# Moving GpSimd's Newton steps, weight splits and gate split within the steps of an attention loop

## The chip, the cores and the metric

The kernel runs on one core of a Trainium2 chip. The metric is the device time of one execution in microseconds (us), the median of the runs shown; lower is better.

## What is computed

One layer of a decoder trunk, batch 1, 512 tokens, width 1024, all in float32. Cut to what matters here:

```python
h = rms_norm(x, attn_norm)
(mq, mk, mv, nsq, kc, vc, ksl, vsl, kwn, vwn, ngate, mgate) = split(h @ w_in)
q_a = rms_norm(to_heads(mq, 8), moba_q_gain)      # each head of 64 is normalised by itself
k_a = rms_norm(to_heads(mk, 8), moba_k_gain)
y_a = moba_attention(q_a, k_a, to_heads(mv, 8))    # 8 heads, all causal blocks at this length
q_b = rms_norm(nsq in 8 heads, nsa_q_gain)
y_b = nsa_attention(q_b, ...)                      # 8 heads: compressed, selected and window branch
g_a, g_b = split(sigmoid(mgate))
x = x + (g_a * (y_a @ w_br_moba) + g_b * (y_b @ w_br_nsa)) @ w_o
x = x + (gelu(conv(rms_norm(x) @ w_up)) * lin) @ w_down
x = x + sigmoid(x @ w_ple_gate) * (p @ w_ple)
```

## The kernel before

Each engine (TensorE, VectorE, ScalarE, GpSimd, and SyncE for the DMA queue) has its own instruction stream, in an order written out by hand; semaphores join them. Every float32 matmul is done as three matmuls of a high and a low part (lines 1511 to 1513, in the helper `three`), so each weight has to be split: ScalarE copies a rounded high part, and VectorE or GpSimd subtracts it from the raw weight to get the low part.

The attention half is a loop over 100 steps t. A step is one block of 128 queries of one head and branch. Steps come in pairs of heads: pairs 0 to 3 have 8 steps each (t = 0, 8, 16, 24 are their first), pairs 4 to 7 have 17 each (first steps 32, 49, 66, 83). In step t TensorE computes `scores(t)`, transposes the probabilities of step t-3 (`turn_probs`, line 1660), and between them does a few matmul rows of other work:

- `project`: the projection h @ w_in of a *weight unit* w, four token tiles of 128 rows, 8 rows of k each. Unit w=3 is projected in steps 4 to 9, unit 4 in steps 12 to 17, unit 5 in 20 to 25, unit 6 in 28 to 35 and unit 7 in 43 to 58. Each unit gives the queries, keys and values of a later pair.
- `gate`: one of 16 column blocks of the merge gates.
- `turn_tile` (line 1571): the transposes of a normalised tile of queries and keys, in step TURN.

The other engines' part of a step:

- VectorE: `bias(t)` (line 1295, adds the bias strip and takes the minimum), `invert(t-1)` (line 1312), `sums` of squares (line 1229), `pt_low` (line 1330), `tile_low` (line 1281, low parts of the tile turned a step before), `w_low` (line 1171, even rows of the unit's weights), `normalise` (line 1262, of one tile), `guess` (lines 1146 to 1148, three small instructions that make a first guess of the inverse square roots of two tiles), `gate_low` (line 1187, the first half of a gate's low part), and every so often a copy of a finished output (line 1402).
- ScalarE: takes projected tiles from PSUM (line 830), `pt_high` (line 919), `tile_high` (line 883), `exp(t)` (line 894), a gate's tanh (line 926) and high part (line 1000), and the high parts of two rows of weights (line 835).
- GpSimd: `scale(t-1)` (lines 706 and 709, multiplies the probabilities by 1/sum), `split_gate` (line 674, the second half of a gate's low part), `split_unit` (line 670, the odd rows of the unit's weights), `v_low` (lines 683 and 688, the low part of the values), and `root` (lines 719 to 725): three Newton rounds of four instructions on 8 columns, which turn the guess into the inverse roots that `normalise` needs.

Planning dictionaries say in which step each thing falls. Before the change GUESS and ROOT are one: VectorE's `guess` and GpSimd's `root` stand in the same step. The roots of a unit are done in two halves of two token tiles. The step of ROOT is 0 and 2 for unit 2; 7 and 10, 15 and 18, 23 and 26 for units 3, 4, 5; 32 and 36 for unit 6; 51 and 59 for unit 7. `split_gate` stands in steps 4, 12, 20, 28, 40, 48, 57 and later. SPLIT has the rows 0-1, 2-3, 4-5, 6-7 of unit 3 in steps 1 to 4, of unit 4 in steps 9 to 12, of unit 5 in steps 17 to 20, of unit 6 in steps 25 to 28, of unit 7 in steps 41 to 44.

TensorE asks for row 7 of the weights (the last one that GpSimd splits) in the second step of a unit's projection, and before `turn_tile` it waits for `norm_done`. A projected tile is taken from PSUM only when the same tile of the unit before is normalised. SyncE's queue waits, in the step of `split_gate`, for both halves of that split before it loads the weights of the gate after.

Of the kernel before, what the change touches and what calls it, by code (L numbers as in the profile page):

```python
# [35 lines left out]
NGATE = 2 * D // P  # L36
# [36 lines left out]
def layer(nc, A, out):  # L73
# [20 lines left out]
    GATE, j = {}, 2  # L94
# [14 lines left out]
                j += 1  # L109
    gate_end = {j: t for t, (j, kts) in GATE.items() if kts[-1] == KT - 1}  # L110

    PROJ, SPLIT, VALUES, ROOT, TILE, TURN = {}, {}, {}, {}, {}, {}
    ROWS = NT * KT
    for w in range(2, W_UNITS):
        b0 = first_t[w - 2]
        if w == 2:
            start, counts, row = b0, (4, 4), ROWS - KT
        elif w < 6:
            start, counts, row = b0 - 4, (5, 6, 5, 5, 6, 5), 0
        elif w == 6:  # L120
            start, counts, row = b0 - 4, (4,) * 8, 0
        else:
            start, counts, row = b0 - 6, (2,) * 16, 0
        for a, count in enumerate(counts):
            PROJ[start + a] = (w, row, row + count)
            row += count
        split0 = b0 - 8 if w == 7 else b0 - 7
        for a in range(KT // 2):
            SPLIT[split0 + a] = (w, range(2 * a, 2 * a + 2))
        VALUES[start + len(counts)] = w  # L130
        ends = [t for t in sorted(PROJ) if PROJ[t][0] == w for r in range(*PROJ[t][1:]) if r % KT == KT - 1]
        for half in range(2):
            t = ends[2 * half + 1] + 1 if w > 2 else b0 + 2 * half
            ROOT[t] = (w, half)
            for a in range(2):
                TILE[t + 1 + half + 2 * a], TURN[t + 2 + half + 2 * a] = (w, 2 * half + a), (w, 2 * half + a)

    def segments(t):

# [58 lines left out]
    with ExitStack() as ctx:  # L198
# [453 lines left out]
        def _(pool):  # L652
# [19 lines left out]
            def split_gate(j):  # L672
                pool.wait_ge(g_hi, j + 1)
                pool.tensor_tensor(Gl[:, 4:8, :], graw[:, 4:8, :], Gh[:, 4:8, :].bitcast(F32), ALU.subtract).then_inc(g_lo[1], 1)  # L674
# [17 lines left out]
            def split_chunk(c):  # L692
                pool.wait_ge(w2_hi, c + 1)
                pool.tensor_tensor(W2l[:, c % RING, :], raw2[:, c % RING, :], W2h[:, c % RING, :].bitcast(F32),  # L694
                                   ALU.subtract).then_inc(w2_lo, 1)
# [12 lines left out]
                    h = cat(s["br"]) * HN + 2 * (s["n"] - 4) + s["e"]  # L708
                    pool.tensor_scalar(p_, p_, r, gsig[:, s["i"], h:h + 1], ALU.mult, ALU.mult).then_inc(scaled, 1)  # L709

            def root(w, half):

                number = 2 * (w - 2) + half
                c = slice(8 * half, 8 * half + 8)
                y, v, a = rq[:, c], st[:, 40:56][:, c], st[:, 60:76][:, c]
                pool.wait_ge(guess_done, number + 1)
                for i in range(3):
                    done = 12 * number + 4 * i
                    pool.tensor_tensor(a, y, y, ALU.mult).then_inc(root_done, 1)
                    pool.wait_ge(root_done, done + 1)  # L720
                    pool.tensor_tensor(a, a, v, ALU.mult).then_inc(root_done, 1)
                    pool.wait_ge(root_done, done + 2)
                    pool.tensor_scalar(a, a, -0.5, 1.5, ALU.mult, ALU.add).then_inc(root_done, 1)
                    pool.wait_ge(root_done, done + 3)
                    pool.tensor_tensor(y, y, a, ALU.mult).then_inc(root_done, 1)
                    if i < 2:
                        pool.wait_ge(root_done, done + 4)
# [36 lines left out]
            for t in range(T + 1):  # L764
                if t >= 1:
                    scale(t - 1)
                if t == T:
                    break
                for j, end in gate_end.items():
                    if t == end + 1 and j + 1 < NGATE:  # L770
                        split_gate(j + 1)
                if t in SPLIT:
                    split_unit(*SPLIT[t])
                if t in VALUES and VALUES[t] != 6:
                    v_low(VALUES[t])
                if t in ROOT:
                    root(*ROOT[t])
                if t in EARLY:
                    split_chunk(EARLY[t])

# [348 lines left out]
        def _(dve):  # L1129
# [116 lines left out]
            def guess(w, half):  # L1246

                c = slice(8 * half, 8 * half + 8)
                dve.wait_ge(ss_done, NT * (w - 2) + 2 * half + 2)
                if w > 2:  # L1250
                    dve.wait_ge(norm_done, norm_number(w - 1, 2 * half + 1))
                first_guess(rq[:, c], st[:, 40:56][:, c], st[:, 60:76][:, c], ss[:, c], 1.0 / DH, guess_done)
# [118 lines left out]
            for t in range(T + LAG):  # L1371
                n, k, w = (STEPS[t]["n"], STEPS[t]["k"], STEPS[t]["n"] + 2) if t < T else (NPAIR, 0, 0)
# [11 lines left out]
                    w_low(*SPLIT[t])  # L1384
                if t in TILE:
                    normalise(*TILE[t])
                if t in ROOT:
                    guess(*ROOT[t])
                for j, end in gate_end.items():
                    if t == end + 1 and j + 1 < NGATE:  # L1390
                        gate_low(j + 1)
# [15 lines left out]
            for mg in range(2):  # L1407
# [5 lines left out]
                for m in range(4):  # L1413
                    i = 4 * mg + m
# [7 lines left out]
                for m in range(4):  # L1422
                    i = 4 * mg + m
# [8 lines left out]
            for mg in range(2):  # L1432
                for m in range(4):
                    i = 4 * mg + m
# [48 lines left out]
            for mg in range(2):  # L1483
                for m in range(4):
                    i = 4 * mg + m
# [449 lines left out]
```

## Time and profile before

| | before |
|---|---|
| median of 3 runs | 942.68 us (942.12 to 945.08) |
| the profiled execution | 943.29 us |
| its span, first to last instruction | 941.3 us |
| TensorE busy | 894.5 us, 95% of the span |
| VectorE, ScalarE, GpSimd busy | 438.2, 410.6, 434.4 us |
| mean granted clock of TensorE | 0.985 |

The profiled execution is one run; its time is 2 us more than its span. Times inside the trace are from the span's start. An engine's idle time before an instruction is shown with what ended it, in square brackets.

### The profile page before, as it was taken

The numbers are of one execution on the slowest core, as the hardware profiler recorded it, in microseconds if no ns is written. First come the engines' busy times: TensorE is split into PE (matmuls) and PEld (weight loads), VectorE is DVE, ScalarE is ACT, GpSimd is POOL, SyncE is SP. The second block draws the span as 40 slices with busy tenths as digits, with TensorE's granted clock in tenths as the row PEclk, the third lists the DMA queues.
The fourth block names the chain that finished last, engine by engine and source line by source line (L and its number), as shares of the span: only waits on it lengthen the run. The fifth ranks groups of instructions, "written<-read, shape, count | busy, mean of one in ns | idle before, by whom it ended". The sixth has DMA issues, their size and how long they took to land.

```text
span 941.3 us, 13367 instructions
## 1 busy us (share of the span) xinstructions
PE 894.5 (95%) x4585; PEld 769.2 (82%) x4585; DVE 438.2 (47%) x965; ACT 410.6 (44%) x889; POOL 434.4 (46%) x557
## 2 busy tenths in 40 slices
PE   6898989998999799999999999999999999999998
PEld 6897888987889688878778788888888888888886
DVE  5718558658666464563431743333344441021134
ACT  4221546546565455572343474444444443232231
POOL 4633445535443433475446164444444445444450
PEclk7998999999999999999999999999999999999999
DMA  5744324224112122616653163333333233332213
GB/s 168 164 132 118 82 84 94 71 85 105 42 34 68 34 81 65 213 46 235 201 190 101 51 197 101 104 104 94 101 96 95 90 101 101 101 100 89 91 57 134
DMA packets 101365, 99.33 MB, mean 106 GB/s; under 512 B 15956, under 2 KB 76084, under 8 KB 101300
## 3 DMA queue, kind: packets, MB, share of 16 engines
q1 hardware_dynamic: 101247, 98.48, 35.7%
q8 instruction: 38, 0.62, 0.3%
q14 instruction: 27, 0.22, 0.1%
q10 hardware_dynamic: 53, 0.01, 0.0%
HBM read 87.58 MB, written 10.88 MB: 105 GB/s over the span
## 4 chain that ended last, share of the span: by engine, by line
PE 79%; DVE 9%; POOL 3%; issue 3%; ACT 3%; DMA 2%; SPq 1%; DVEq 0%; ACTq 0%; POOLq 0%
PE banks L1511 24%; PE banks L1512 23%; PE banks L1513 23%; PE banks L1660 2%; PE banks L1640 1%; PE banks L1639 1%; DVE plain_arena L1262 1%; PE banks L1571 1%; DVE split_arena L1281 1%; DMA plain_arena<-in_x_dram 1%; PE banks L1597 1%; DMA plain_arena<-in_w_in_dram 1%; POOL split_arena L670 1%; ACT split_arena L1000 1%; DVE split_arena L1187 1%
## 5 line engine op out<-in xcount | busy, mean ns | idle before, releaser
L1511 PE MATMUL banks<-split_arena 128*128 128x512 f32 (+4 forms) x1228 | 466.2, 380 | 17.1 <-POOL split_arena L670 7.2
L1513 PE MATMUL banks<-split_arena 128*128 128x512 f32 (+4 forms) x1228 | 455.4, 371 | 0.0
L1512 PE MATMUL banks<-split_arena 128*128 128x512 f32 (+4 forms) x1228 | 455.2, 371 | 0.0
L694 POOL TENSOR_TENSOR split_arena<-plain_arena,split_arena 128x512 fp32r<-128x512 f32 x184 | 241.2, 1323 | 254.4 <-ACT split_arena L935 235.1
L1511 PEld LDWEIGHTS banks<-split_arena 128*128 128x128 f32 x1228 | 232.3, 189 | 58.5 <-POOL split_arena L670 9.3
L1513 PEld LDWEIGHTS banks<-split_arena 128*128 128x128 f32 x1228 | 232.3, 189 | 35.5
L1512 PEld LDWEIGHTS banks<-split_arena 128*128 128x128 f32 x1228 | 232.7, 190 | 32.0
L935 ACT ACTIVATE split_arena<-plain_arena 128x512 fp32r<-128x512 f32 x184 | 113.0, 627 | 192.7 <-PE banks L1513 177.3
L1469 DVE SCALAR_TENSOR_TENSOR plain_arena<-banks,plain_arena 128x511 f32<-128x511 f32 x44 | 32.7, 743 | 133.2 <-ACT plain_arena L1040 133.2
L894 ACT ACTIVATE plain_arena<-plain_arena 128x128 f32<-128x128 f32 (+1 forms) x96 | 53.9, 562 | 65.0 <-DVE plain_arena L1295 64.5
L709 POOL TENSOR_SCALAR plain_arena<-plain_arena 128x128 f32<-128x128 f32 (+1 forms) x64 | 40.7, 636 | 72.7 <-DVE plain_arena L1312 72.5
L1295 DVE CUSTOM_DVE_ANT_0 plain_arena<-banks,plain_arena 128x128 f32<-128x128 f32 (+1 forms) x96 | 46.7, 487 | 51.0 <-PE banks L1640 50.2
L919 ACT ACTIVATE split_arena<-banks 128x128 fp32r<-128x128 f32 (+1 forms) x96 | 41.4, 431 | 64.1 <-PE banks L1660 55.4
L1330 DVE TENSOR_TENSOR split_arena<-banks,split_arena 128x128 fp32r<-128x128 f32 (+1 forms) x96 | 46.3, 482 | 16.4 <-ACT split_arena L919 14.9
L1660 PE MATMUL banks<-plain_arena 128*128 128x128 f32 x240 | 43.2, 278 | 6.9 <-POOL plain_arena L709 4.7
L1487 DVE TENSOR_TENSOR plain_arena<-banks,plain_arena 128x512 f32<-128x512 f32 x8 | 5.0, 684 | 86.5 <-PE banks L1513 86.5
L670 POOL TENSOR_TENSOR split_arena<-plain_arena,split_arena 128x384 fp32r<-128x384 f32 (+1 forms) x28 | 31.9, 1141 | 26.9 <-DVE split_arena L1164 14.6
L1040 ACT ACTIVATE plain_arena<-banks,plain_arena 128x512 f32<-128x512 f32 x44 | 30.7, 778 | 22.3 <-PE banks L1513 22.3
L674 POOL TENSOR_TENSOR split_arena<-plain_arena,split_arena 128x512 fp32r<-128x512 f32 x16 | 27.7, 1734 | 26.4 <-DVE split_arena L1182 14.4
L706 POOL TENSOR_SCALAR plain_arena<-plain_arena 128x128 f32<-128x128 f32 (+3 forms) x32 | 17.7, 553 | 46.5 <-DVE plain_arena L1312 46.4
L1660 PEld LDWEIGHTS banks<-plain_arena 128*128 128x128 f32 x240 | 28.6, 142 | 9.9 <-POOL plain_arena L709 6.9
L1471 DVE SCALAR_TENSOR_TENSOR plain_arena<-banks,plain_arena 128x510 f32<-128x510 f32 x44 | 33.0, 749 | 1.5
(170 smaller groups left out, 835.5 us busy)
## 6 DMA issues: line engine op xcount, KB each, us to landing
plain_arena<-in_w_up_dram SPq DMA_DIRECT2D x88, 256.0 KB, 3.1
plain_arena<-in_w_down_dram SPq DMA_DIRECT2D x44, 256.0 KB, 2.6
plain_arena<-in_w_in_dram SPq DMA_DIRECT2D x18, 512.0 KB, 4.5
plain_arena<-in_w_in_dram SPq DMA_DIRECT2D x32, 192.0 KB, 3.5
plain_arena<-in_x_dram SPq DMA_DIRECT2D x8, 512.0 KB, 5.2
gates<-plain_arena SPq DMA_DIRECT2D x16, 256.0 KB, 2.0
plain_arena<-skew SPq DMA_DIRECT2D x16, 256.0 KB, 4.0
plain_arena<-gates SPq DMA_DIRECT2D x16, 256.0 KB, 3.7
```

Source lines behind the costliest of these rows:

```text
L670: pool.tensor_tensor(Wl[:, kt, 0:c], raw[:, kt, 0:c], Wh[:, kt, 0:c].bitcast(F32), ALU.subtract).then_inc(w_lo[1], 1)
L694: pool.tensor_tensor(W2l[:, c % RING, :], raw2[:, c % RING, :], W2h[:, c % RING, :].bitcast(F32), ALU.subtract).then_inc(w2_lo, 1)
L709: pool.tensor_scalar(p_, p_, r, gsig[:, s["i"], h:h + 1], ALU.mult, ALU.mult).then_inc(scaled, 1)
L894: nc.scalar.activation(prob[:, t % 4, 0:nk], prob[:, t % 4, 0:nk], ACT.Exp, bias=mneg[:, t % 4:t % 4 + 1], scale=-1.0, accum_out=rsum[:, t ...
L919: nc.scalar.activation(PTh[:, s["u"] % 2, 0:i + 1, P * i:P * (i + 1)], PS[:, 4 + t % 2, 0:P * (i + 1)].rearrange("p (j q) -> p j q", j=i + ...
L935: nc.scalar.activation(W2h[:, c % RING, :], raw2[:, c % RING, :], ACT.Copy).then_inc(w2_hi, 1)
L1295: nc.vector.tensor_tensor_reduce(out=prob[:, t % 4, 0:nk], in0=PS[:, 2 + t % 2, 0:nk], in1=strip[:, n % 2, e, S - nk:S], scale=1.0, scalar ...
L1330: nc.vector.tensor_tensor(PTl[:, s["u"] % 2, 0:i + 1, P * i:P * (i + 1)], PS[:, 4 + t % 2, 0:P * (i + 1)].rearrange("p (j q) -> p j q", j= ...
L1511: nc.tensor.matmul(o, ah, bh, start=first, stop=False)
L1512: nc.tensor.matmul(o, ah, bl, start=False, stop=False)
L1513: return nc.tensor.matmul(o, al, bh, start=False, stop=last)
L1660: ins = nc.tensor.transpose(PS[:, 4 + t % 2, P * j:P * (j + 1)], prob[:, t % 4, P * j:P * (j + 1)], ident)
```

## The change

`root` gets a step of its own, one after `guess`. For the second half of units 2 to 5 it is cut in two: round 0 in the step after the guess, rounds 1 and 2 in the one after that (`late`). The steps of `normalise` (TILE) and `turn_tile` (TURN) follow:

| unit, half | guess | root, before and after | TILE before | TILE after |
|---|---|---|---|---|
| 2, first | 0 | 0, 1 | 1, 3 | 2, 4 |
| 2, second | 2 | 2, 3 and 4 | 4, 6 | 5, 7 |
| 3, first (4 and 5: 8 and 16 more) | 7 | 7, 8 | 8, 10 | 9, 11 |
| 3, second (4 and 5: 8 and 16 more) | 10 | 10, 11 and 12 | 12, 14 | 13, 15 |
| 6, first | 32 | 32, 33 | 33, 35 | 34, 36 |
| 6, second | 36 | 36, 37 | 38, 40 | 38, 40 |
| 7, first | 51 | 51, 52 | 52, 54 | 53, 55 |
| 7, second | 59 | 59, 60 | 61, 63 | 61, 63 |

TURN is one step after TILE, as before. Within a step GpSimd's order becomes scale, weights, values, root, gate's half, early chunk; before it was scale, gate's half, weights, values, root, early chunk. No instruction is added or removed.

```diff
@@ planning
         for half in range(2):
             t = ends[2 * half + 1] + 1 if w > 2 else b0 + 2 * half
-            ROOT[t] = (w, half)
+            GUESS[t] = (w, half)
+            late = 1 if half and w < 6 else 0
+            if late:
+                ROOT[t + 1], ROOT[t + 2] = (w, half, range(1)), (w, half, range(1, 3))
+            else:
+                ROOT[t + 1] = (w, half, range(3))
             for a in range(2):
-                TILE[t + 1 + half + 2 * a], TURN[t + 2 + half + 2 * a] = (w, 2 * half + a), (w, 2 * half + a)
+                TILE[t + 2 + late + 2 * a], TURN[t + 3 + late + 2 * a] = (w, 2 * half + a), (w, 2 * half + a)
@@ GpSimd
-            def root(w, half):
+            def root(w, half, rounds):
...
-                for i in range(3):
+                for i in rounds:
@@ GpSimd's loop over the steps
-                for j, end in gate_end.items():
-                    if t == end + 1 and j + 1 < NGATE:
-                        split_gate(j + 1)
                 if t in SPLIT:
                     split_unit(*SPLIT[t])
                 if t in VALUES and VALUES[t] != 6:
                     v_low(VALUES[t])
                 if t in ROOT:
                     root(*ROOT[t])
+                for j, end in gate_end.items():
+                    if t == end + 1 and j + 1 < NGATE:
+                        split_gate(j + 1)
@@ VectorE's loop over the steps
-                if t in ROOT:
-                    guess(*ROOT[t])
+                if t in GUESS:
+                    guess(*GUESS[t])
```

## Rows read from the trace of the kernel before

**Rows 1.** The page's first part: busy us (share of the span) xinstructions.
```profile
PE 894.5 (95%) x4585; PEld 769.2 (82%) x4585; DVE 438.2 (47%) x965; ACT 410.6 (44%) x889; POOL 434.4 (46%) x557
```

**Rows 2.** Waits of PE, 100 to 400 us: us in total, times, longest.
```profile
PE banks L1511 <- POOL split_arena L670: 7.2, 5, 1.7
```

**Rows 3.** Timeline of PE, 103 to 266 us: start, us, instruction, idle before.
```profile
120.01 0.44 PE L1511 MATMUL banks<-split_arena 128*128 128x384 f32 x1 [0.29 <-DVE split_arena L1171]
122.55 0.45 PE L1511 MATMUL banks<-split_arena 128*128 128x384 f32 x1 [1.75 <-POOL split_arena L670]
...
157.81 0.44 PE L1511 MATMUL banks<-split_arena 128*128 128x384 f32 x1 [1.67 <-POOL split_arena L670]
...
227.41 0.39 PE L1511 MATMUL banks<-split_arena 128*128 128x256 f32 x1 [1.65 <-POOL split_arena L670]
229.80 0.38 PE L1511 MATMUL banks<-split_arena 128*128 128x256 f32 x1 [0.55 <-ACT plain_arena L830]
241.87 0.38 PE L1511 MATMUL banks<-split_arena 128*128 128x256 f32 x1 [0.50 <-ACT plain_arena L830]
244.81 0.63 PE L1571 MATMUL banks<-plain_arena 128*128 128x128 f32 x4 [0.55 <-DVE plain_arena L1262]
...
256.37 0.63 PE L1571 MATMUL banks<-plain_arena 128*128 128x128 f32 x4
```

**Rows 4.** Timeline of POOL, steps 10 to 12, ahead of the wait at 157.81.
```profile
148.94 0.20 POOL L719 TENSOR_TENSOR plain_arena<-plain_arena 128x8 f32<-128x8 f32 x1 [0.31 <-DVE plain_arena L1148]
...
152.36 0.20 POOL L725 TENSOR_TENSOR plain_arena<-plain_arena 128x8 f32<-128x8 f32 x1
...
153.10 1.02 POOL L670 TENSOR_TENSOR split_arena<-plain_arena,split_arena 128x384 fp32r<-128x384 f32 x1
...
154.76 1.60 POOL L674 TENSOR_TENSOR split_arena<-plain_arena,split_arena 128x512 fp32r<-128x512 f32 x1
156.31 1.44 POOL L670 TENSOR_TENSOR split_arena<-plain_arena,split_arena 128x384 fp32r<-128x384 f32 x1
```

**Rows 5.** Timeline of ACT: high parts of rows 6 and 7, units 3 and 4.
```profile
118.49 0.92 ACT L835 ACTIVATE split_arena<-plain_arena 128x384 fp32r<-128x384 f32 x2
...
153.89 0.94 ACT L835 ACTIVATE split_arena<-plain_arena 128x384 fp32r<-128x384 f32 x2
```

**Rows 6.** Timeline of DVE: a guess, three normalises, and an invert (L1312).
```profile
147.45 1.21 DVE L1147 TENSOR_SCALAR plain_arena<-plain_arena 128x8 int32<-128x8 int32 x1
...
225.01 1.76 DVE L1262 TENSOR_TENSOR plain_arena<-plain_arena 128x512 f32<-128x512 f32 x1
...
243.98 0.69 DVE L1262 TENSOR_TENSOR plain_arena<-plain_arena 128x512 f32<-128x512 f32 x1 [2.54 <-POOL plain_arena L725]
...
252.22 0.16 DVE L1312 RECIPROCAL plain_arena<-plain_arena 128x1 f32<-128x1 f32 x1
...
321.49 0.69 DVE L1262 TENSOR_TENSOR plain_arena<-plain_arena 128x512 f32<-128x512 f32 x1 [4.61 <-POOL plain_arena L725]
```

**Rows 7.** Timeline of POOL, steps 59 to 62.
```profile
315.35 2.82 POOL L688 TENSOR_TENSOR split_arena<-plain_arena,split_arena 128x256 fp32r<-128x256 f32 x4 [1.64 <-ACT split_arena L866]
318.13 0.20 POOL L719 TENSOR_TENSOR plain_arena<-plain_arena 128x8 f32<-128x8 f32 x1
...
321.45 2.38 POOL L709 TENSOR_SCALAR plain_arena<-plain_arena 128x384 f32<-128x384 f32 x3
```

**Rows 8.** Timeline of PE: step 62, and a long wait near the start.
```profile
45.55 1.73 PE L1563 MATMUL banks<-plain_arena 128*128 128x128 f32 x8 [3.05 <-DVE plain_arena L1222]
...
322.69 0.90 PE L1660 MATMUL banks<-plain_arena 128*128 128x128 f32 x3 [4.66 <-POOL plain_arena L709]
...
324.67 1.05 PE L1571 MATMUL banks<-plain_arena 128*128 128x128 f32 x4
```

**Rows 9.** Windows: us, busy of PE, PEld, DVE, ACT, POOL, clock, DMA, GB/s.
```profile
322.30:325.70 3.40, 3.01 (x11) 2.62 (x12) 0.86 (x4) 0.98 (x3) 1.52 (x3) 0.50 0.00 0
...
332.50:336.00 3.50, 3.50 (x15) 3.21 (x15) 2.95 (x9) 3.00 (x7) 1.06 (x2) 0.51 0.13 50
```

More of the change, by code:

```diff
@@ L110, in layer @@
     gate_end = {j: t for t, (j, kts) in GATE.items() if kts[-1] == KT - 1}
-    PROJ, SPLIT, VALUES, ROOT, TILE, TURN = {}, {}, {}, {}, {}, {}
+    PROJ, SPLIT, VALUES, GUESS, ROOT, TILE, TURN = {}, {}, {}, {}, {}, {}, {}
     ROWS = NT * KT
```

## The prediction

> **What bounds the kernel now.** I read the busy times first, then TensorE's waits between 100 and 400 us (steps 0 to 64, the only part that the change touches), then for each wait that involves GpSimd the timelines of the four engines around it. TensorE is busy for 894.5 of 941.3 us [rows 1], so an edit on another engine is worth what it takes from TensorE's idle time, and no more. In the part touched, the largest kind of wait is the matmul's for a weight row that GpSimd splits: five times, 7.2 us together [rows 2]. Four of them are of one pattern, 1.65 to 1.75 us each, in the second step of the projection of units 3, 4, 5 and 6; three of the four stand in [rows 3], unit 5's is as unit 4's, 35 us later. The largest single wait is 4.66 us, for a scaled block of probabilities in step 62 [rows 8]. Both kinds end in GpSimd's program order. The rows of GpSimd in steps 10 to 12 show it: the root's twelve instructions hold it from 148.94 to 152.56 us, then comes the rest in a row, the gate's half (1.60 us) ahead of the weight row (1.44 us), which ends at 157.75 [rows 4], and TensorE starts at 157.81 [rows 3]. In step 59 the root sits between `v_low` and `scale(59)` [rows 7]; TensorE needs the latter.
>
> **The change part by part.** No work is added, so each part is a shift, and I follow what is late next.
>
> *Units 4 and 5, row 7.* With the gate's half behind the weights and a third of the root (3.62 / 3 = 1.2 us) left in step 11, GpSimd has more than 3 us less ahead of row 7. What is late next is ScalarE's high part of that row: 153.89 + 0.94 = 154.83 us [rows 5]. I put it at 155.1, since `bias(12)` now has a normalise ahead of it on VectorE (about 0.7 us more), while a `tile_high` leaves ScalarE's step 12. The split takes between 1.02 us and 1.44 us [rows 4], so row 7 is there at 156.1 to 156.5, and TensorE would ask at 157.81 - 1.67 = 156.14. Gain 1.3 to 1.67 us; I take 1.5 for each unit, 3.0 us.
>
> *Unit 3.* Shorter waits stand ahead of it, one of them at 120.01, and they partly merge: ScalarE's high parts of rows 6 and 7 are ready at about 118.95 and 119.41 [rows 5]. Row 6 is split by VectorE and reaches TensorE at 120.01 now [rows 3], and no earlier after the change. Row 7 can then be there at 119.41 + 1.02 or 1.44 = 120.4 to 120.9 in place of 122.55. Gain 1.65 to 2.1, I take 1.85 us.
>
> *Unit 6.* The wait of 1.65 us goes in the same way, but behind it stands one of 0.55 us for ScalarE's taking of a projected tile [rows 3], which hangs on VectorE: normalise, gate's low part, output copy, bias(29), then exp(29), then the tile. The normalise in that row started at 225.01 and took 1.76 us [rows 6]; it leaves step 28. From its end to the matmul at 229.80 are 3.03 us; counted from its start instead, the matmul can begin at 228.04. Gain 1.5 us (at most 1.76). Full removal of all three waits there would need more than this chain allows.
>
> *Unit 6, first half of the roots.* VectorE now waits 2.54 us for the root in step 33 [rows 6], and TensorE waits 0.50 and 0.55 us behind it [rows 3]. With root in step 33 and normalise in step 34, bias(33) and bias(34) run ahead of the wait. Gain 1.0 us, between 0 and 1.05.
>
> *Unit 6, second half: a loss.* Here the guess stays in step 36 and normalise in step 38, but the root goes behind `scale(36)`, which waits for the invert at 252.22 [rows 6]. Invert 0.16, scale 0.5 (estimate: a third or less of the 1.60 for a block of 128x512), twelve small instructions 3.3 us, as from 318.13 to 321.45 [rows 7], normalise 0.7: the tile is ready at about 256.9, while TensorE turns it at 256.37 now, without a wait [rows 3]. Loss 0.6 us, between 0 and 0.9.
>
> *Unit 7, second half.* `v_low` ends at 318.13, and root runs from there to 321.45 [rows 7]. After the change `scale(59)` goes first: 318.15 to 318.85 (estimate: 2.38 us for three of them [rows 7]), so TensorE's transposes start at about 318.9 in place of 322.69. But root then ends at 318.85 + 3.3 = 322.15, normalise ends at 322.85, and `turn_tile`, in the same step 62 just behind one gate row, waits for it until 322.95 instead of starting at 324.67 [rows 8]. So of the 4.66 us wait only a piece of 1.7 us goes; the rest moves from `turn_probs` to `turn_tile`, and VectorE's wait at 321.49 [rows 6] gets 0.7 us longer. The clock makes it less: from 322.3 to 325.7 us TensorE ran at a granted clock of 0.50, that is 1.2 GHz [rows 9], right behind the wait. If that fall comes after the change too, TensorE has done at 325.7 us work worth (325.7 - 322.95) / 2 = 1.4 us beyond the start of the turn, against (325.7 - 324.67) / 2 = 0.5 now: a gain of 0.9 us. Without the fall it is 2.3. An idle of 3.05 us near the start was also followed by a fall (the row at 45.55), and after the change some 0.85 + 2.9 us of idle lie in 4.9 us; so I take 0.9.
>
> On this the Trainium skill ("TensorE: Matmul & The Clock Gate", section "What's actually happening") says that the clock is gated down when the array has been idle and let up by activity. The rows agree as far as they go; by that rule a wait cut in two by a microsecond of work might keep the clock up, which is a rival below.
>
> *At nothing.* The first halves of units 2, 3, 4, 5 and 7: the root goes one step later and normalise and turn with it; TensorE's own projection rows, several us a step, cover it. Were that cover gone, each would cost the root's length, 3.3 us. The gate's half ends 3 to 4 us later in steps 4, 12, 20 and 28. SyncE's queue waits for it before it loads the next gate's weights, with no other load of that step behind it, and TensorE asks for this half six steps later; without that cover it would be 4 times 3.6 us. `tile_high` falls into step 9's, 17's and 25's ScalarE queue, at most 0.2 us ahead of a gate's start. The steps from 65 on have the same order as before.
>
> Small instructions that meet big ones: a guess's second instruction took 1.21 us [rows 6] beside GpSimd's splits, six times the 0.20 of one of GpSimd's own small ones [rows 4]. Moving twelve such instructions of GpSimd beside other VectorE work can cost some tenths each way; I leave this in the range.
>
> Sum: 3.0 + 1.85 + 1.5 + 1.0 - 0.6 + 0.9 = 7.65 us. The profiled execution took 943.29 us, 0.6 above the median of 942.68; 943.29 - 7.65 = 935.6, and on the median 935.0 us.
>
> **The rivals.** A difference of 0.3% (2.8 us, so under 939.9 or over 945.5) is about what a measurement of this kernel can tell.
>
> - *The clock does not fall (0.17).* The idle in step 62 is split by turn_probs and a gate row. If the fall at 322.3 does not come, 1.4 us more are won; if the second stretch at half clock, 332.5 to 336.0 [rows 9], goes too, up to 1.75 more, since TensorE is busy for all of its 3.5 us. Time 932 to 933.6, with the upper ends of the other terms down to 930.5. For it: the longest wait shrinks. Against it: the fall behind 3.05 us.
> - *The waits change their names (0.18).* ScalarE's high part of row 7 comes later than I reckon, because bias(12) and exp(12) are behind one more normalise and tile_low in step 11. At 1 us later in each of units 3 to 6, 4 us are lost again: 939.0.
> - *No effect (0.10).* The same at 1.5 to 1.7 us, the whole wait, with the gains of unit 7 eaten by unit 6's second half: 940.5 to 943.
> - *Slower (0.05).* VectorE runs in order, and a normalise that waits for a root holds back bias, exp, scale and so the transposes: that is what made 4.61 us on VectorE into 4.66 on TensorE [rows 6, 8]. Rounds 1 and 2 now stand behind a weight row that waits for ScalarE. In units 4 and 5 the root is done by 156.5 + 2.4 = 158.9 (eight of its twelve instructions), and VectorE has the gate's low part, a copy, bias(13) and a tile_low to do before it asks. It decides once the root ends some 2 us later than that: then bias(14) is held back. Twelve halves moved, at 1 us each: 12 lost against 7.65 won, 947.
>
> **How the numbers follow.** The forecast itself (gains of 6 to 9 us, 933.6 to 936.7) has 0.50. The likeliest time is 935.0. Faster: 0.50 + 0.17 + 0.18 = 0.85, same 0.10, slower 0.05. The range goes from 930.5, where every term is at its upper end and the clock falls once less, to 939.5; below it I leave 0.03 and above it 0.16.
>
> **What would show it.** (1) The waits of L1511 for L670 between 100 and 240 us fall from 7.2 us to under 1.5. (2) In step 12 GpSimd runs row 7's split right behind ScalarE's copy, and the gate's half after eight root instructions. (3) At unit 6's second half a new wait of some 0.6 us at L1571 for the normalise. (4) In step 62 two waits, about 0.9 us at L1660 and 2 to 3 us at L1571 for L1262. (5) After step 65 the same busy time and order, shifted. The prediction is wrong if TensorE waits for ScalarE's weight copies or VectorE's row 6 in place of GpSimd's, or if VectorE begins to wait for L725 in units 3 to 5 and its bias comes late.

## The result, and the profile after

| | before | changed |
|---|---|---|
| median, runs made together | 943.23 us (6 runs, 941.31 to 945.08) | 935.13 us (6 runs, 933.13 to 935.68) |
| the profiled execution, its span | 943.29 us, 941.3 us | 935.20 us, 933.4 us |
| TensorE busy | [rows 1] | 891.5 us, 96% |
| mean granted clock of TensorE | 0.985 | 0.988 |

The ratio is 0.9911, with a 95% interval of 0.9895 to 0.9928: the changed kernel is faster by 0.7% to 1.05%. Forecast were 935.0 us and a range of 930.5 to 939.5. Two single executions of kernels below, one of 1785.22 us (e2_root_later) and the profiled one of e3_unit2_as_before with 1480.71 us, are in no median here and no trace of theirs is used.

TensorE's waits in the touched part (100 to 400 us), from the waits view of the changed kernel. Columns: who waits, for which line, us in total, times, longest. The lines of helpers are five higher than before.

```profile
PE banks L1516 <- DVE split_arena L1192: 6.2, 5, 1.5
PE banks L1576 <- DVE plain_arena L1267: 4.7, 3, 2.9
PE banks L1516 <- DVE split_arena L1176: 3.1, 2, 1.7
PE banks L1516 <- ACT plain_arena L835: 1.6, 5, 0.6
PE banks L1665 <- DVE split_arena L1335: 1.5, 2, 0.7
PE banks L1665 <- POOL plain_arena L714: 0.8, 1, 0.8
PE banks L1516 <- POOL split_arena L675: 0.7, 1, 0.7
```

The last line answers to [rows 2]: 0.7 us where there were 7.2. But two names are large that were not: VectorE's weight rows (L1176, 3.1 us) and its normalised tiles (L1267, 4.7 us). TensorE's own rows say where they stand. This is its timeline in the changed kernel, answering to [rows 3] and [rows 8]:

```profile
115.51 0.44 PE L1516 MATMUL banks<-split_arena 128*128 128x384 f32 x1 [1.37 <-DVE split_arena L1176]
119.14 0.44 PE L1516 MATMUL banks<-split_arena 128*128 128x384 f32 x1 [1.74 <-DVE split_arena L1176]
120.60 0.45 PE L1516 MATMUL banks<-split_arena 128*128 128x384 f32 x1 [0.67 <-POOL split_arena L675]
...
221.26 0.39 PE L1516 MATMUL banks<-split_arena 128*128 128x256 f32 x1 [0.37 <-ACT plain_arena L835]
223.37 0.63 PE L1576 MATMUL banks<-plain_arena 128*128 128x128 f32 x4 [0.40 <-DVE plain_arena L1267]
248.50 0.63 PE L1576 MATMUL banks<-plain_arena 128*128 128x128 f32 x4 [1.40 <-DVE plain_arena L1267]
...
311.16 0.55 PE L1665 MATMUL banks<-plain_arena 128*128 128x128 f32 x3 [0.84 <-POOL plain_arena L714]
315.26 1.09 PE L1576 MATMUL banks<-plain_arena 128*128 128x128 f32 x4 [2.87 <-DVE plain_arena L1267]
328.33 0.50 PE L1516 MATMUL banks<-split_arena 128*128 128x512 f32 x1 [1.42 <-DVE split_arena L1192]
```

Unit 3 (115 to 121 us) still waits, now for VectorE. In the second projection step of units 4 and 5 nothing of a wait is left. Unit 6 keeps 0.4 us, and has a new wait of 1.40 at its second half. In step 62 the 4.66 us of [rows 8] have become 0.84 and 2.87. The last row is a wait in step 66 for VectorE's part of a gate's low half, which the trace of before doesn't have: it makes the first line of the waits 6.2 us in five where it was 4.7 in four.

A wait's listed idle isn't the whole of what it costs, so the account is better made from fixed points. The table gives how much earlier than before TensorE's first matmul of `scores(t)` starts in the changed kernel, each profiled execution from its own start. The difference of two columns is what was won between the two steps.

| step t | 0 | 8 | 16 | 24 | 32 | 36 | 44 | 61 | 76 |
|---|---|---|---|---|---|---|---|---|---|
| us earlier | 1.22 | 1.35 | 3.36 | 5.34 | 8.09 | 9.29 | 7.70 | 7.73 | 8.08 |

At step 98 it is 8.09, so nothing moves after step 76. The 1.22 us at step 0 lie ahead of anything that the change moves. They are a difference of the start-up between one program or execution and another: the kernel below that moves only the gate's half has 2.72 there, the one that moves only the root 0.83. From step 0 to the end the trace credits 8.08 - 1.22 = 6.9 us to the change.

Two columns hold some bookkeeping. With the change the turn of unit 2's last tile moves from step 7 to step 8 and that of unit 5's last from step 31 to step 32, so there is one `turn_tile` less between steps 0 and 8 and one more between 32 and 36. Such a turn takes about 0.4 us (from 132.07 to 132.50 us in the trace of before). On equal work the 0.13 us won between steps 0 and 8 are a loss of 0.3, and the 1.20 between 32 and 36 are 1.6.

### The profile page after: what moved, and what is told of

Its sections match the earlier page's. It is cut to its first block, busy times and chain, and to the rows that moved or that the text cites. A ratio compares the mean times of both kernels' runs of the same rounds, so it can differ in the third digit from the quotient of the medians.

```text
span 933.4 us, 13371 instructions
## 1 busy us (share of the span) xinstructions
PE 891.5 (96%) x4585; PEld 768.7 (82%) x4585; DVE 432.1 (46%) x965; ACT 411.8 (44%) x889; POOL 438.0 (47%) x557
## 4 chain that ended last, share of the span: by engine, by line
PE 82%; DVE 7%; ACT 4%; issue 3%; POOL 3%; DMA 1%; SPq 0%; DVEq 0%; ACTq 0%; POOLq 0%
PE banks L1516 25%; PE banks L1517 24%; PE banks L1518 24%; PE banks L1665 2%; PE banks L1645 1%; PE banks L1644 1%; PE banks L1576 1%; DMA plain_arena<-in_x_dram 1%; PE banks L1602 1%; ACT split_arena L1005 1%; PE banks L1533 1%; DVE plain_arena L1300 1%; DMA plain_arena<-gates 1%; DVE split_arena L1169 1%; DVE split_arena L1192 1%
## 5 line engine op out<-in xcount | busy, mean ns | idle before, releaser
L711 POOL TENSOR_SCALAR plain_arena<-plain_arena 128x128 f32<-128x128 f32 (+3 forms) x32 | 21.4, 670 | 53.3 <-DVE plain_arena L1317 52.9
```

## The experiments

Each kernel is compared with executions of the kernel before made together with it; `before` had medians of 943.41 us (17 executions, with the first four kernels below), 942.26 (11, with the next two) and 945.22 (9, with the last two), so ratios are compared, not times. "Won between steps" is read as in the table above, always against the trace of before.

### One part alone: the gate's half last, and the root later

The kernel before with only `split_gate` moved behind `root` (e1_gate_last):

```diff
-                for j, end in gate_end.items():
-                    if t == end + 1 and j + 1 < NGATE:
-                        split_gate(j + 1)
                 if t in SPLIT:
...
                     root(*ROOT[t])
+                for j, end in gate_end.items():
+                    if t == end + 1 and j + 1 < NGATE:
+                        split_gate(j + 1)
```

> The kernel before with one edit: GpSimd does the gate's half behind weights, values and root in its step; guess, root, normalise and turn stay where they were. Theory 'order': in units 3 to 6 the last weight row only queued behind the gate's half (1.60 us), and the root alone leaves it late by little. The four waits of L1511 for L670 (7.2 us) fall to under 1.5 us, about 2 us won in each of units 4 and 5, 1.5 to 2.5 in units 3 and 6, none at unit 7 (the wait of 4.66 us stays). 6 to 8 us under before, that is 935 to 937, so most of what the whole change gave. Theory 'root': the twelve root instructions ahead are what makes the row late, and the order in the step matters little: 940 to 942.

The changed kernel with the gate's half first again, the same edit backwards (e2_root_later):

> The changed kernel with the gate's half put back in front of the weights; root, normalise and turn stay later. Theory 'order': with root a step later, the gate's half still starts only when ScalarE's copy is there and takes 1.60 us ahead of the row, so the waits of L1516 for L675 stay at 1 us or so each; with the gains at unit 7 and losses at units 2 and 6 the kernel ends 1 to 4 us under before, 939 to 942. Theory 'root': 936 or less, the waits of units 4 and 5 gone.

Measured: the gate's half alone 940.0 us, ratio 0.9968 (0.9951 to 0.9984); the root's part alone 935.82 us (five executions, 934.54 to 938.21), ratio 0.9913 (0.9886 to 0.994), which can't be told from the whole change's 0.9911. Won between steps:

| | 0 to 8 | 8 to 16 | 16 to 24 | 24 to 32 | 32 to 44 | 61 to 76 |
|---|---|---|---|---|---|---|
| gate's half alone | -0.04 | 1.71 | 1.65 | -1.38 | -0.03 | -0.68 |
| root's part alone | -0.34 | 1.43 | 1.40 | 2.85 | -0.38 | 1.56 |
| both (the change) | 0.13 | 2.01 | 1.98 | 2.75 | -0.39 | 0.35 |

Each theory was half right. The time of the gate's half alone is that of "root" (940 to 942), though its two gains in units 4 and 5 are near those of "order"; the root's part alone met "root" in both. In units 4 and 5 either part alone removes most of the wait, and the two don't add up. GpSimd had some 3 us too many ahead of row 7 where 1.7 would have been enough. In unit 6 the gate's half alone wins nothing. TensorE's waits in that kernel:

```profile
122.30 0.66 PE L1571 MATMUL banks<-plain_arena 128*128 128x128 f32 x4 [1.76 <-DVE split_arena L1281]
...
223.76 0.38 PE L1511 MATMUL banks<-split_arena 128*128 128x256 f32 x1 [2.03 <-ACT plain_arena L830]
...
318.07 0.90 PE L1660 MATMUL banks<-plain_arena 128*128 128x128 f32 x3 [4.66 <-POOL plain_arena L709]
```

The wait for GpSimd's row at unit 6 has become one of 2.03 us for the projected tile, the one of 0.55 us in [rows 3] grown by what stood before it, and behind it the granted clock is 0.50 for 3.4 us, which takes the rest of the 1.38 us lost. So the chain that the prediction named there (normalise, bias, exp, tile) is what keeps unit 6 late, and only the later normalise loosens it. The wait in step 62 is untouched at 4.66. The order inside GpSimd's step is thus the small part of this change.

### Unit 2 left as it was, and the last tiles a step later

Two kernels from the changed one, and one with both edits. First, unit 2's root, normalise and turn put back where they were before (e3_unit2_as_before):

```diff
-            late = 1 if half and w < 6 else 0
-            if late:
+            late = (half - 1 if w == 2 else 1 if half and w < 6 else 0)
+            if w == 2:
+                ROOT[t] = (w, half, range(3))
+            elif late:
```

> The changed kernel, but unit 2's roots, tiles and turns keep the steps of the kernel before. In the changed kernel's trace VectorE waits 2.36 us for unit 2's first root, its next guess then sticks behind GpSimd's splits, bias(3) comes 0.9 us late and TensorE waits 1.37 and 1.74 us for weight rows that VectorE splits. Theory: with unit 2 as before these waits shrink to 0.3 each and unit 3 gets the 1.85 us that were forecast: 1.5 to 2.5 us under the changed kernel, 932.6 to 933.6. Rival: the waits come from ScalarE's weight copies anyhow, and the time stays within 0.5 us of the changed kernel.

Second, TILE and TURN of the second halves of units 6 and 7 one step later (e4_tiles_later):

```diff
-                TILE[t + 2 + late + 2 * a], TURN[t + 3 + late + 2 * a] = (w, 2 * half + a), (w, 2 * half + a)
+                after = t + 2 + max(late, half if w > 5 else late) + 2 * a
+                TILE[after], TURN[after + 1] = (w, 2 * half + a), (w, 2 * half + a)
```

> The changed kernel, but for the second halves of units 6 and 7 normalise and turn come one step later still. Theory: the waits at the turns (1.40 and 2.87 us) go, because the tiles are not asked for before the next head pair, and the stretch of 6.8 us at half clock behind the second goes or shrinks: 4 to 7 us under the changed kernel, 928 to 931. Rival: TensorE then waits elsewhere in the same steps for scale or bias, which hang on the same root, and only 0 to 2 us are won.

Both edits together (e5_both):

> Unit 2 as in the kernel before, and for units 6 and 7 the tiles of the second half one step later: the two edits tried alone, together. The first gained some 1.8 us and the second some 2.4 us in the medians. If they are independent (unit 2 lies at 100 to 130 us, the others behind 240 us): 930.5 to 932, and in the trace no wait of over 1 us between 100 and 120 us. Rival: what the second edit won was only the clock, by chance of the run, and the pair gives 1 to 2 us under the changed kernel, 933.5 to 934.

Measured: 933.32 us, ratio 0.9891 (0.9863 to 0.9919); 932.71 us, 0.989 (0.9863 to 0.9917); 932.46 us, 0.9901 (0.9876 to 0.9926). All three intervals overlap that of the change, so the times alone decide nothing here. The first is where its theory had it (932.6 to 933.6), the second short of its 928 to 931, the pair between its theory (930.5 to 932) and its rival. Of the first there is no usable trace; the kernel with both edits shows what it does in unit 3:

```profile
113.44 0.45 PE L1519 MATMUL banks<-split_arena 128*128 128x384 f32 x1 [0.34 <-DVE split_arena L1179]
115.53 0.55 PE L1668 MATMUL banks<-plain_arena 128*128 128x128 f32 x3 [0.52 <-POOL plain_arena L714]
116.50 0.44 PE L1519 MATMUL banks<-split_arena 128*128 128x384 f32 x1 [0.42 <-POOL split_arena L678]
117.58 0.44 PE L1519 MATMUL banks<-split_arena 128*128 128x384 f32 x1 [0.29 <-DVE split_arena L1179]
122.59 0.65 PE L1579 MATMUL banks<-plain_arena 128*128 128x128 f32 x4 [1.77 <-DVE split_arena L1289]
```

The waits for weights are small, as expected, but a transposed tile now waits 1.77 us for VectorE, as at 122.30 in the kernel with the gate's half alone. Between steps 0 and 8 this kernel wins -0.05 us, and 2.52 between 8 and 16, with unit 2's last turn in step 7 again; together 2.47, against 2.14 in the change. Putting unit 2 back mostly exchanges one wait for another and is worth 0.3 us: that version of the theory fell, although the time had met it.

The tiles a step later moved the wait in step 62 and left its size. TensorE and GpSimd there, in that kernel (lines one more than in the changed kernel):

```profile
316.37 0.66 PE L1666 MATMUL banks<-plain_arena 128*128 128x128 f32 x4 [2.96 <-POOL plain_arena L715]
```

```profile
311.10 0.67 POOL L715 TENSOR_SCALAR plain_arena<-plain_arena 128x384 f32<-128x384 f32 x1
311.72 0.20 POOL L725 TENSOR_TENSOR plain_arena<-plain_arena 128x8 f32<-128x8 f32 x1
...
314.83 0.20 POOL L731 TENSOR_TENSOR plain_arena<-plain_arena 128x8 f32<-128x8 f32 x1
315.02 2.27 POOL L715 TENSOR_SCALAR plain_arena<-plain_arena 128x512 f32<-128x512 f32 x3
```

At unit 6 it was the same: the turn's 1.40 us became 1.46 for the scale (L715) and 1.78 for a later normalise, and the loss between steps 36 and 44 grew from 1.59 to 2.18 us. No longer the turn waits for the normalise (2.87 us), but `turn_probs` for the scale behind the root (2.96 us). The root itself, 315.02 - 311.72 = 3.3 us in one piece, is what is late, whoever waits. That led to the next kernel.

### The root spread over three steps

To the kernel with both edits: the second halves of units 6 and 7 get one Newton round a step in three steps, and their tiles two steps later than in the change (e6_spread):

```diff
+            if half and w > 5:
+                for i in range(3):
+                    ROOT[t + 1 + i] = (w, half, range(i, i + 1))
...
-                after = t + 2 + max(late, half if w > 5 else late) + 2 * a
+                after = t + 2 + max(late, 2 * half if w > 5 else late) + 2 * a
```

> As the kernel of the pair, but in the second halves of units 6 and 7 the three Newton rounds go into three steps, one round (four instructions, 1.1 us) each, and normalise and turn follow another step later. With tiles later alone, the wait at unit 7 moved to the transposes of step 60's probabilities (2.96 us for L715), since scale(60) stands behind all twelve root instructions (3.3 us) in steps without projection work. Theory: it is the root's length ahead of scale that TensorE waits for; with one round a step the wait of 2.96 us shrinks to at most 1 us, the one of 1.46 us at unit 6 to under 0.5, and another 2 to 3.5 us are won: 927.5 to 930. Rival: VectorE's order (the normalise blocking bias) is what counts, and the time stays within 1 us of the pair.

Measured: 929.44 us (929.18 to 929.65), ratio 0.9858 (0.9836 to 0.988). TensorE and GpSimd in steps 60 to 62:

```profile
308.23 0.55 PE L1671 MATMUL banks<-plain_arena 128*128 128x128 f32 x3 [0.84 <-POOL plain_arena L720]
310.13 0.66 PE L1671 MATMUL banks<-plain_arena 128*128 128x128 f32 x4 [0.31 <-POOL plain_arena L720]
```

```profile
309.00 0.20 POOL L736 TENSOR_TENSOR plain_arena<-plain_arena 128x8 f32<-128x8 f32 x1
309.30 0.77 POOL L720 TENSOR_SCALAR plain_arena<-plain_arena 128x512 f32<-128x512 f32 x1
...
310.90 0.20 POOL L736 TENSOR_TENSOR plain_arena<-plain_arena 128x8 f32<-128x8 f32 x1
311.20 0.45 POOL L720 TENSOR_SCALAR plain_arena<-plain_arena 128x128 f32<-128x128 f32 x1
```

Between two scales lies one round of four small instructions, and the wait of 2.96 us is 0.31. Between steps 61 and 76 this kernel wins 5.27 us, against 0.35 in the change; 3.1 us of the difference is the clock, as shown further below, since the kernel with only the tiles later wins 3.49 there. At unit 6 the loss between steps 36 and 44 is 0.56 us, against 1.59 in the change and 2.22 with both edits. The tiles went one step further here too; that this step alone would do nothing for a wait behind `scale` follows from GpSimd's order, but wasn't run.

### The two programs once more

The changed kernel (e7_changed_again) and the one before (e8_before_again), one profile of each, to see what of the traces repeats.

> The changed kernel, profiled once more, to see what differs between two executions of one program. Theory: the schedule between 100 and 310 us repeats within 0.3 us, but the stretches at half clock do not: the one behind the waits of unit 7 is 3.4 or 6.8 us long or absent, and the time from step 61 to step 76 differs by 1 to 3 us. Rival: the clock falls at the same place for the same length, and the trace is the same.

> The kernel before, profiled once more, for the same question: waits of 1.65 to 1.75 us four times and of 4.66 us once come back within 0.1 us; the number of stretches at half clock may differ. If it does, the gain at unit 7 is a number of the pair of runs and not of the kernels.

Measured: 936.54 and 943.97 us, and the rival came: the stretches at half clock stand in the same places with the same lengths in steps 61 to 76, one of 6.8 us in the changed kernel (from 314.3 and from 313.1 us) and two of 3.4 us in the one before. The kernel before repeats to 0.15 us at each of the steps of the table. The changed one has 1.52, 1.65, 3.67, 5.65 and 8.62 us at steps 0, 8, 16, 24 and 32: the same gains up to step 24, 2.97 in place of 2.75 between 24 and 32, and 0.64 in place of 0.35 between 61 and 76. So differences of a few tenths between traces mean nothing, and the two us at units 4 and 5 do. The start-up repeats as well, 0 and -0.07 us in the kernel before, 1.22 and 1.52 in the changed one: it goes with the program rather than the execution. What makes it differ, when no instruction that was moved has run by then, stays open.

### Unit 3: who holds VectorE back

The changed kernel with the spread roots and nothing else of the above (e9_spread_only), and the same with unit 2's four tiles in steps 3, 4, 5, 6 in place of 2, 4, 5, 7 (e10_tiles_3_to_6):

```diff
+                if w == 2:
+                    after = 3 + 2 * half + a
                 TILE[after], TURN[after + 1] = (w, 2 * half + a), (w, 2 * half + a)
```

> The changed kernel with the second halves of the roots of units 6 and 7 spread over three steps (a round in each, tiles two steps later), and unit 2 left as the change puts it. The kernel that also puts unit 2's roots and tiles back took 929.44 us. Theory A (unit 2's later root costs unit 3 most of its expected gain, 1.7 us): this kernel takes about 931 us, and the starts of scores between steps 8 and 16 move by less than in that kernel. Theory B (unit 2's place is worth nothing, one wait in unit 3 is only exchanged for another): within 0.7 us of 929.4, and the starts of scores(61) and scores(98) differ by 5.3 us more against the kernel before at the end than at step 61, as there.

> As the run beside it, but unit 2's four tiles are normalised in steps 3, 4, 5 and 6 and turned in 4 to 7, in place of 2, 4, 5, 7 and 3, 5, 6, 8, so that no normalise stands in the step right behind its root, the first of them a whole step later. Theory A (in the changed kernel VectorE waits 2.36 us at 109.80 for the root of step 1, its guess follows late and beside GpSimd's splits, and ScalarE's weight copies with it, which makes the waits of 1.37 and 1.74 us in step 4): the wait at VectorE goes, the two waits in step 4 shrink by at least 1.5 us together, and the kernel is 1 to 1.8 us faster than the run beside it. Theory B (what is late in step 4 is ScalarE's copy whatever VectorE does before): the two waits stay near 3 us together and the times agree within 0.5 us.

Measured: 930.37 us (928.13 to 932.43), ratio 0.984 (0.9815 to 0.9864), and 927.01 us (925.61 to 928.77), ratio 0.9802 (0.978 to 0.9825). The first is what spreading is worth on top of the change: 5.26 us won between steps 61 and 76 in place of 0.35. Whether unit 2's old place adds to it stays open: the traces say 0.9 us up to step 16 (2.51 won against 1.57), the ratios 0.9858 and 0.984 say the reverse, and their intervals overlap. Of the 0.9 some 0.6 is the clock: in e9_spread_only the granted clock is 0.50 from 120.8 to 124.2 us, and between steps 0 and 8 it wins -0.45 us where the change, with the same order there and no such stretch, wins 0.13.

The second answers the question of unit 3. VectorE in the changed kernel:

```profile
109.80 0.69 DVE L1267 TENSOR_TENSOR plain_arena<-plain_arena 128x512 f32<-128x512 f32 x1 [2.36 <-POOL plain_arena L730]
110.41 0.37 DVE L1151 TENSOR_SCALAR plain_arena<-plain_arena 128x8 f32<-128x8 f32 x1
110.81 0.94 DVE L1152 TENSOR_SCALAR plain_arena<-plain_arena 128x8 int32<-128x8 int32 x1
111.79 1.21 DVE L1153 TENSOR_SCALAR plain_arena<-plain_arena 128x8 int32<-128x8 int32 x1
112.91 0.68 DVE L1300 CUSTOM_DVE_ANT_0 plain_arena<-banks,plain_arena 128x512 f32<-128x512 f32 x1
```

GpSimd beside it in the same kernel:

```profile
109.56 0.20 POOL L730 TENSOR_TENSOR plain_arena<-plain_arena 128x8 f32<-128x8 f32 x1
109.75 1.00 POOL L711 TENSOR_SCALAR plain_arena<-plain_arena 128x256 f32<-128x256 f32 x1
110.72 1.00 POOL L675 TENSOR_TENSOR split_arena<-plain_arena,split_arena 128x384 fp32r<-128x384 f32 x1
111.69 1.28 POOL L688 TENSOR_TENSOR split_arena<-plain_arena,split_arena 128x512 fp32r<-128x512 f32 x1
```

And VectorE in the kernel with tiles in steps 3 to 6 (lines six more), with TensorE's waits of its unit 3 below:

```profile
107.06 0.17 DVE L1157 TENSOR_SCALAR plain_arena<-plain_arena 128x8 f32<-128x8 f32 x1
107.27 0.17 DVE L1158 TENSOR_SCALAR plain_arena<-plain_arena 128x8 int32<-128x8 int32 x1
107.47 0.17 DVE L1159 TENSOR_SCALAR plain_arena<-plain_arena 128x8 int32<-128x8 int32 x1
108.06 0.69 DVE L1306 CUSTOM_DVE_ANT_0 plain_arena<-banks,plain_arena 128x512 f32<-128x512 f32 x1 [0.41 <-PE banks L1651]
```

```profile
116.27 0.44 PE L1522 MATMUL banks<-split_arena 128*128 128x384 f32 x1 [0.85 <-DVE split_arena L1182]
118.14 0.45 PE L1522 MATMUL banks<-split_arena 128*128 128x384 f32 x1 [1.07 <-POOL split_arena L681]
125.02 0.66 PE L1582 MATMUL banks<-plain_arena 128*128 128x128 f32 x4 [0.38 <-DVE split_arena L1292]
```

In the change a normalise stands in the step behind its root. VectorE waits for it, the guess behind it runs into GpSimd's large instructions, and its last two small ones end within 0.1 us of a GpSimd instruction's end (111.75 beside 111.72, 113.00 beside 112.97). Then the bias starts at 112.91, where the other kernel has it at 108.06, and exp and ScalarE's weight copies follow it. With the normalise one step later the three instructions take 0.17 us each, and the waits for weights in unit 3 fall from 3.78 us to 1.92. Between steps 0 and 8 this kernel wins 1.85 us, against 0.13 in the change and -0.45 (with the stretch at half clock) in the kernel beside it. Over the whole kernel it is 3.4 us faster than the latter in the medians, more than the 1 to 1.8 expected, and 2.8 from step 0 on in the traces, 0.6 of them the clock's. How much of it is VectorE's wait and how much the slow small instructions, the two runs don't separate.

The Trainium skill ("SBUF — State Buffer", section "Who interferes with whom") has GpSimd share a pair of ports with VectorE: when a VectorE instruction is in a mode that uses both pairs, as a `tensor_scalar` can be, whichever of the two engines issues first holds the shared pair for its whole instruction, and the other is blocked. The ends at 111.75 and 113.00 agree with that; no run here shows in which mode these instructions ran.

## Why the prediction came out as it did

The time was met, 935.13 against 935.0, and the likeliest case was the one that came. The terms, as won between steps:

| term | predicted | measured |
|---|---|---|
| unit 3 (steps 0 to 8) | 1.85 | 0.13 |
| units 4 and 5 (8 to 24) | 3.0 | 3.99 |
| unit 6, its three waits (24 to 32) | 1.5 | 2.75 |
| unit 6, first half of the roots (32 to 36) | 1.0 | 1.20 |
| unit 6, second half (36 to 44) | -0.6 | -1.59 |
| unit 7, second half (61 to 76) | 0.9 | 0.35 |
| sum | 7.65 | 6.83 |
| start-up, ahead of step 0 | 0 | 1.22 |

- *Units 4 and 5* (right, undersized). GpSimd splits row 7 right behind ScalarE's copy and the remaining eight root instructions and the gate's half come after, as in sign (2); TensorE doesn't wait. The margin that kept the rival "slower" away was not the reckoned 2 us but nothing: the root ended at 156.48, and VectorE, done with its other work at 156.41, had come to ask for it. More than the listed 1.67 was won because a listed idle leaves out what the overlap of matmuls loses. Ahead of the wait in [rows 3] the trace of before has this; the numbers in front are start and length:

```profile
155.62 0.33 PE L1512 MATMUL banks<-split_arena 128*128 128x384 f32 x1
155.80 0.34 PE L1513 MATMUL banks<-split_arena 128*128 128x384 f32 x1
157.81 0.44 PE L1511 MATMUL banks<-split_arena 128*128 128x384 f32 x1 [1.67 <-POOL split_arena L670]
158.09 0.34 PE L1512 MATMUL banks<-split_arena 128*128 128x384 f32 x1
```

  Starts are 0.18 us apart in a full stream, but 2.01 and then 0.28 here: 2.01 - 0.18 + 0.28 - 0.18 = 1.93 us lost, close to the 2.01 and 1.98 measured.
- *Unit 3* (wrong by 1.7 us, 2.1 on equal work, the term of the sum that was mis-sized most). The step that failed: "The first halves of units 2, 3, 4, 5 and 7: the root goes one step later and normalise and turn with it; TensorE's own projection rows, several us a step, cover it." That was put at nothing for unit 2. In its short first steps VectorE, not TensorE, was what had no cover, and ScalarE's rows 6 and 7, taken to stay at 118.95 and 119.41, came 0.7 us later relative to the start of the steps (ready at 118.91, where 119.41 less the 1.22 us of start-up is 118.19). A second thing was left out: with unit 2's root as before and row 7's wait gone, TensorE waited 1.77 us for `tile_low` and nothing was won either. It is the case that the end of the prediction names, TensorE waiting for VectorE's row in place of GpSimd's. The last experiment won back the whole term, 1.85 us.
- *Unit 6, start* (right in kind, low, and above the "at most 1.76" of the prediction). The whole of 1.65 + 0.55 us went but for 0.37 and 0.40 us listed, two smaller waits ahead of them went too (0.21 at 223.49 and 0.34 at 225.14 us in the trace of before), and the overlap again makes up the rest. That the tile's chain, not GpSimd's row, was binding is shown by the kernel with the gate's half alone.
- *Unit 6, first half* (right in kind, low). 1.20 for 1.0, and 1.6 on equal work: both listed waits of 0.50 and 0.55 went, with what their overlap cost.
- *Unit 6, second half* (sign right, 1.0 us too small). From the invert of step 36 to the end of the normalise 4.7 us were reckoned (252.22 to 256.9) and 4.73 measured (243.62 to 248.35). What was missed is that the invert itself is later: the first half's second normalise, 0.69 us at 241.46, moved from step 35 into step 36, ahead of the bias. The wait is 1.40 where 0.6 was expected, and the clock isn't in it.
- *Unit 7* (mechanism right, size a question of the clock). `turn_probs` waits 0.84 us and `turn_tile` 2.87, against "about 0.9" and "2 to 3" in sign (4), and VectorE waits 5.26 us, 0.65 longer than in [rows 6] where 0.7 was expected. The clock fell behind it for 6.8 us, twice the 3.4 us that follow the wait in [rows 9]. The windows view (columns as in [rows 9]) of the changed kernel, and of the one with tiles a step later, whose two waits were 0.84 and 2.96:

```profile
310.90:314.30 3.40, 1.24 (x6) 0.77 (x6) 0.00 (x0) 0.49 (x1) 2.49 (x13) 1.00 0.00 0
314.30:321.10 6.80, 5.84 (x19) 4.99 (x20) 4.59 (x14) 2.96 (x9) 2.37 (x4) 0.50 0.00 0
```

```profile
312.00:316.00 4.00, 1.41 (x8) 0.96 (x7) 1.49 (x3) 0.98 (x3) 3.16 (x12) 1.00 0.00 0
316.30:323.10 6.80, 6.73 (x44) 6.03 (x45) 4.54 (x13) 3.44 (x10) 1.65 (x4) 1.00 0.00 0
```

  Ahead of both the array was busy for about a third of the time (1.24 of 3.40 us, 1.41 of 4.00); behind it the granted clock is 0.50 in the one and 1.00 in the other. Five profiled executions had nearly this pair of waits. The change and its repetition had 6.8 us at half clock (0.35 and 0.64 us won between steps 61 and 76), the root alone and the kernel with both edits 3.4 us (1.56 and 1.86), and the tiles a step later none (3.49). The spread kernels, with 0.31 us in place of the second wait, had no fall and won 5.27 and 5.26. The rival "the clock does not fall" thus stands for some 3 us in this place, but the change as made didn't get it, and that this equals the reckoned 1.4 and 1.75 is chance. The second stretch of [rows 9], from 332.5 us, is gone in every kernel but the one before, and it was worth nothing: in the change 1.5 us are won by the start of step 66 and lost again in it, in the wait of 1.42 us at 328.33. In the kernel before TensorE came to that matmul late, after a step 65 at half clock, and VectorE was done. The 3.1 us lie in the stretch of 6.8 us behind the turn.
- *Signs.* (1) and (2) as said, (3) with 1.40 for 0.6, (4) as said, (5) as said from step 67 on (8.08 us at step 76 and 8.09 at step 98), but with the new wait in step 66.
- *The rivals.* "The waits change their names" happened in unit 3 only, through VectorE and not through tile_low; "slower" nowhere, though only just: the root of unit 4 is done at 156.48 and normalised at 156.52.

So the sum was met by errors of both signs: unit 3, unit 6's second half and unit 7 took 1.7 + 1.0 + 0.55 = 3.3 us off, units 4 and 5 and the rest of unit 6 put 1.0 + 1.25 + 0.2 = 2.4 on. The median's gain of 8.1 us is 1.2 more than the trace credits to the change. The trace has those 1.2 ahead of step 0, and the second profile of each program repeats them, but nothing in the change explains them. That the median fell 0.1 us beside the forecast is therefore luck; the mechanism was right for units 4 to 7 and wrong for unit 3.

## What to carry to other kernels

When a long run of small instructions on one engine gates another, moving it past the urgent work exchanges one wait for the next (4.66 us became 0.84 and 2.87, then 2.96 elsewhere); cutting it into pieces between the urgent instructions left 0.84 and 0.31. A consumer that waits in its own stream belongs well behind its producer (one step was too little in the short first steps, two were enough), even where what it makes isn't needed soon, because all that is queued behind it waits too. Cost a moved instruction also in the step that it moves into: the 0.7 us of a normalise ahead of a bias came back as TensorE's wait.

## What the runs showed of the hardware that had not been expected

- VectorE's instructions on 8 columns took 0.17 us beside GpSimd's small ones and 0.94 and 1.21 us beside its 1.00 and 1.28 us ones, ending within 0.1 us of them.
- A wait of 1.67 us by the trace cost TensorE about 1.9 to 2.0 us.
- The stretch at half clock (1.2 GHz) behind almost the same idle was 6.8, 3.4 or 0 us long from one kernel to another, worth up to 3.1 us of time here; for the same program it came back the same (6.8 us from 314.3 and from 313.1).
- The end of a stretch at half clock need not give its time back: 1.5 us won by step 66 went into a wait of 1.42 us that the slow matmuls before had covered.
